# Seven block products instead of eight for the gate projection of a merge stage

## The chip, the cores and the metric

The kernel runs on one core of a Trainium2 chip, in float32 throughout. The metric is the device time of one execution in microseconds (us). PE is TensorE, PEld its weight loads, DVE VectorE, ACT ScalarE, POOL GpSimd, SP the engine whose queue issues most DMAs.

## The reference

A trunk of two layers over 512 latent tokens (layer 0 also carries 256 context tokens, so 768 in all; layer 1 has 512). Each layer runs a normalisation, a Hyena branch and an attention branch side by side, merges them, and then runs a mixture of experts. The change touches the merge alone:

```python
def merge_branches(p_gate, y_hy, y_att, w_hy_o, w_mla_o, w_out):
    g = jax.nn.sigmoid(p_gate)
    return (g[..., :D_MODEL] * (y_hy @ w_hy_o) + g[..., D_MODEL:] * (y_att @ w_mla_o)) @ w_out
```

`p_gate` is the normalised input `u` (tokens x 1024) times the last 2048 columns of `w_in`. `y_hy` and `y_att` have 512 columns each.

## The kernel before

The program is a row of stages. `stage` opens a block in which each engine has its own instruction list, and ends it with a barrier of all engines, so that no stage begins before the one ahead of it has ended on every engine. For each layer the order is: input projections, convolution, attention, merge (`merge_stage`), output projection and router logits (`out_stage`), router, experts.

Everything is held transposed: channels on the 128 partitions, tokens along the free dimension. `merge_stage` makes the 1024 output channels in 8 column chunks of 128, called c below (`KC` is 8). For a chunk it needs 16 weight tiles of 128x128 for the two gates (8 contraction chunks each) and 4 + 4 tiles for the two branch outputs. `merge_loads` fetches those 24 tiles into one of two halves of `w_merge`, in four DMAs. The halves for c = 0 and 1 are loaded during the attention stage; the half for c + 2 is loaded when TensorE has done with c.

For each chunk, TensorE works on each stream of tokens in turn (512 columns, and in layer 0 another 256): 8 + 8 matmuls for the gates and 4 + 4 for the branches, into four PSUM banks. ScalarE takes the sigmoid of the two gate banks (L1707), VectorE multiplies it by the two branch banks (L1719), GpSimd adds the two halves into `mix` (L1730). Two sets of four banks alternate. All of it stands in a `Fori` loop of 4 passes, each with both halves. Near the end SP issues the loads of `w_out`, which the next stage reads.

A float32 matmul shows in the trace as two records, each with a weight load of its own. One chunk is therefore 48 records for each stream.

Of the kernel before, what the change touches and what calls it, by code (L numbers as in the profile page):

```python
# [22 lines left out]
ACT = mybir.ActivationFunctionType  # L23
ALU = mybir.AluOpType
AX = mybir.AxisListType

P = 128
D = 1024
KC = D // P
SEQ, CTX = 512, 256  # L30
# [9 lines left out]
HC = HW // P  # L40
# [76 lines left out]
@contextmanager  # L117
def stage(nc, name, signals, buffers=()):

    with ExitStack() as ctx:  # L120
        mine = {n: ctx.enter_context(nc.sbuf_tensor(f"{name}_{n}", shape, dt[0] if dt else F32))
                for n, shape, *dt in buffers}
        sems = {n: nc.alloc_semaphore(f"{name}_{n}") for n in signals}
        with nc.Block() as block:
            yield block, {**mine, **sems}
        nc.clear_and_free_semaphores(list(sems.values()))
        nc.all_engine_barrier()  # L127
# [1531 lines left out]
def merge_loads(eng, l, i, b, a, early):  # L1659

    w, loaded = early
    for at, n, src, col in ((0, KC, a["w_in"], G0), (KC, KC, a["w_in"], G0 + D), (2 * KC, HC, a["w_hy_o"], 0),
                            (2 * KC + HC, HC, a["w_mla_o"], 0)):
        eng.dma_start(w[:, b, at:at + n], src[l].rearrange("(c p) n -> p c n", p=P)[:, :, bass.ds(i * (2 * P) + (b * P + col), P)]
                      ).then_inc(loaded[b], 16)


def merge_stage(nc, m, l, a, streams, early, then):

    NS = len(streams)  # L1670
    w, loaded = early
    with stage(nc, f"merge{l}", ["mm_done", "sig_done", "prod_done", "mix_done"],
               [("sig", [P, 2, 2, SEQ]), ("t", [P, 2, 2, SEQ])]) as (block, s):
        @block.sync
        def _(sp):
            with sp.Fori(1, KC // 2) as i:
                for b in range(2):
                    sp.wait_ge(s["mm_done"], i * (2 * NS) + (b + 1) * NS)
                    merge_loads(sp, l, i, b, a, early)
            then(sp)  # L1680

        @block.tensor
        def _(pe):
            pe.sem_inc(s["mm_done"], 2 * NS)
            with pe.Fori(0, KC // 2) as i:
                for b in range(2):
                    pe.wait_ge(loaded[b], i * 64 + 64)
                    for t, at, n in streams:
                        k = b * NS + t
                        pe.wait_ge(s["prod_done"], i * (2 * NS) + (k + 1))  # L1690
                        q = 4 * (k % 2)
                        for bank, w_at, z, kn in ((q, 0, m.u, KC), (q + 1, KC, m.u, KC), (q + 2, 2 * KC, m.yh, HC),
                                                  (q + 3, 2 * KC + HC, m.ya, HC)):
                            for c in range(kn):
                                last = nc.tensor.matmul(m.ps[:, bank, 0:n], w[:, b, w_at + c], z[:, c, at:at + n],  # L1695
                                                        start=c == 0, stop=c == kn - 1)
                        last.then_inc(s["mm_done"], 1)

        @block.scalar
        def _(act):  # L1700
            with act.Fori(0, KC // 2) as i:
                for b in range(2):
                    for t, at, n in streams:
                        k = b * NS + t
                        act.wait_ge(s["mm_done"], i * (2 * NS) + (k + 1 + 2 * NS))
                        act.wait_ge(s["prod_done"], i * (2 * NS) + (k + 1))
                        nc.scalar.activation(s["sig"][:, k % 2, :, 0:n], m.ps[:, 4 * (k % 2):4 * (k % 2) + 2, 0:n],  # L1707
                                             ACT.Sigmoid).then_inc(s["sig_done"], 1)

        @block.vector  # L1710
        def _(dve):
            dve.sem_inc(s["prod_done"], 2)  # L1712
            with dve.Fori(0, KC // 2) as i:
                for b in range(2):
                    for t, at, n in streams:
                        k = b * NS + t
                        dve.wait_ge(s["sig_done"], i * (2 * NS) + (k + 1))
                        dve.wait_ge(s["mix_done"], i * (2 * NS) + (k + 1))
                        nc.vector.tensor_tensor(s["t"][:, k % 2, :, 0:n], m.ps[:, 4 * (k % 2) + 2:4 * (k % 2) + 4, 0:n],  # L1719
                                                s["sig"][:, k % 2, :, 0:n], ALU.mult).then_inc(s["prod_done"], 1)  # L1720

        @block.gpsimd
        def _(pool):
            pool.sem_inc(s["mix_done"], 2)
            with pool.Fori(0, KC // 2) as i:
                for b in range(2):
                    for t, at, n in streams:
                        k = b * NS + t
                        pool.wait_ge(s["prod_done"], i * (2 * NS) + (k + 3))
                        nc.gpsimd.tensor_tensor(m.mix[:, bass.ds(i * 2 + b, 1), at:at + n].rearrange("p a n -> p (a n)"),  # L1730
                                                s["t"][:, k % 2, 0, 0:n], s["t"][:, k % 2, 1, 0:n], ALU.add).then_inc(s["mix_done"], 1)


def out_loads(eng, l, w_out, early):
# [132 lines left out]
def mixers(nc, m, l, a, consts, dram, late, begun):  # L1867
# [11 lines left out]
    with ExitStack() as whole, ExitStack() as until_qkv, ExitStack() as until_conv:  # L1879
# [52 lines left out]
        m.mix = late.enter_context(nc.sbuf_tensor(f"mix{l}", [P, KC, TOK], F32, side="right"))  # L1932
        out_early = late.enter_context(nc.sbuf_tensor(f"w_out{l}", [P, 2, KC, 4 * P], F32, side="right")), signals("w_out_in", 2)
        merge_stage(nc, m, l, a, streams, merge_early, lambda sp: out_loads(sp, l, a["w_out"], out_early))
    return out_early

# [682 lines left out]
```

## Time and profile before

| | |
|---|---|
| time, median of 3 runs | 2872.05 us (2866.27 to 2876.56) |
| span of the profiled execution | 2869.8 us |
| PE busy in it | 2557.7 us (89%) |
| DVE, ACT, POOL busy in it | 845.5, 610.8, 516.4 us |
| merge of layer 0, first to last PE record | from 725.7 us, 247.94 us busy |
| merge of layer 1, first to last PE record | from 2059.0 us, 165.06 us busy |

Times in the profile are microseconds from the start of the span. The time of the profiled execution itself, apart from its span, is not recorded; the span lies inside the range of the three runs, 2.25 us under their median.

### The profile page before, as it was taken

To read this page: it belongs to the slowest core of one execution; us is meant where nothing else is said; L and a number is where in the kernel's file an instruction comes from. 1 tells how busy PE (TensorE), PEld (TensorE's weight loads), DVE (VectorE), ACT (ScalarE), POOL (GpSimd) and SP (SyncE) were. 2 spreads that over 40 slices of the span, in tenths; PEclk is the share of its full clock that TensorE was granted. 3 is DMA by queue.
4 is the path that set the end of the run, shared out by engine and by line. 5 is a ranking of instruction groups with operands and counts; after the bars stand their busy time and mean duration, and the time that the engine had idled before them with its cause. 6 is when DMAs were issued, how large, how long until landed. Compare 5 with 4: busy or idle time off the path is not lost. (4 is left out here: it accounts for less than half of the span.)

```text
span 2869.8 us, 33789 instructions
## 1 busy us (share of the span) xinstructions
PE 2557.7 (89%) x12506; PEld 1481.5 (52%) x12506; DVE 845.5 (29%) x1651; ACT 610.8 (21%) x1195; POOL 516.4 (18%) x508
## 2 busy tenths in 40 slices
PE   7997999899999995999888689989999859988886
PEld 2445667555555543555555344755544445555553
DVE  5452257345000135221111142634300242211113
ACT  4342210145000011221111141014300112211111
POOL 0000001166000001222222200116400012222221
PEclk9998999899999997999999889989999979999998
DMA  9872220002023325999999913012033469999996
GB/s 356 294 290 76 74 103 15 20 13 51 23 66 102 125 94 232 388 401 399 402 395 386 357 62 124 30 24 58 1 88 102 182 265 400 389 402 408 400 406 235
DMA packets 208811, 590.78 MB, mean 206 GB/s; under 512 B 47360, under 2 KB 108843, under 8 KB 158412
## 3 DMA queue, kind: packets, MB, share of 16 engines
q1 hardware_dynamic: 185109, 557.75, 51.9%
q0 software_dynamic: 22944, 31.52, 3.3%
q8 instruction: 56, 0.92, 0.1%
q10 hardware_dynamic: 663, 0.27, 0.0%
q14 instruction: 39, 0.32, 0.0%
HBM read 584.07 MB, written 51.51 MB: 221 GB/s over the span
## 5 line engine op out<-in xcount | busy, mean ns | idle before, releaser
L2130 PE MATMUL ps<-w,moe_xt 128*64 128x256 f32 x4096 | 489.0, 393 | 96.4 <-DMA w<-in_w_up_e 94.4
L2130 PEld LDWEIGHTS ps<-w,moe_xt 128*64 128x64 f32 x4096 | 319.9, 141 | 221.1 <-issue 103.2
L2251 POOL DMA_INDIRECT rows_out<-moe_rows_out,table x128 | 118.3, 924 | 736.9 <-DVE moe_rows_out L2313 723.0
L2138 PE MATMUL ps<-w,moe_ht 128*64 128x512 f32 x1024 | 247.8, 605 | 1.6 <-issue 1.6
L2351 DVE TENSOR_TENSOR moe_gated<-ps,moe_gated 64x256 f32<-64x256 f32 x128 | 54.5, 426 | 541.5 <-ACT moe_gated L2332 541.5
L1695 PE MATMUL ps<-u,w_merge 128*128 128x256 f32 (+1 forms) x512 | 167.8, 486 | 2.2 <-DVEq L1712 2.2
L1452 POOL TENSOR_SCALAR attn_p<-attn_p,attn_rs 128x768 f32<-128x768 f32 (+1 forms) x80 | 155.1, 1946 | 81.5 <-DVE attn_rs L1621 81.1
L2313 DVE COPY moe_rows_out<-ps 64x512 f32<-64x512 f32 x128 | 88.7, 693 | 268.2 <-PE ps L2138 268.2
L2332 ACT ACTIVATE moe_gated<-ps 64x256 f32<-64x256 f32 x128 | 48.0, 375 | 549.7 <-PE ps L2130 549.7
L2146 PEld LDWEIGHTS ps<-ident,moe_xg 64*128 64x128 f32 x1024 | 122.5, 200 | 68.2 <-issue 68.2
L2146 PE MATMUL ps<-ident,moe_xg 64*128 64x64 f32 x1024 | 139.9, 277 | 19.1 <-DMA moe_xg<-rows_in,rows 19.0
L1791 PE MATMUL ps<-w_out,mix 128*128 128x512 f32 x320 | 144.6, 612 | 7.7 <-PEq L127 7.7
L1719 DVE TENSOR_TENSOR merge_t<-ps,merge_sig 128x1024 f32<-128x1024 f32 (+1 forms) x24 | 25.1, 1047 | 394.8 <-ACT merge_sig L1707 394.8
L1695 PEld LDWEIGHTS ps<-u,w_merge 128*128 128x128 f32 x512 | 97.2, 190 | 70.4 <-issue 61.2
L948 PE MATMUL ps<-u,w_hy 128*128 128x256 f32 (+1 forms) x384 | 127.1, 491 | 2.7 <-PEq L127 2.7
L2244 POOL DMA_INDIRECT moe_xg<-rows_in,rows x128 | 121.6, 950 | 43.1 <-issue 36.9
L1163 POOL TENSOR_TENSOR conv_u<-conv_u 128x1024 f32<-128x1024 f32 (+1 forms) x12 | 32.7, 2723 | 460.9 <-DVE conv_u L1187 460.9
L1695 PE MATMUL ps<-next_u,w_merge 128*128 128x512 f32 x256 | 111.3, 592 | 1.8 <-DVEq L1712 1.8
L2319 ACT ACTIVATE moe_rows_out<-ps 64x512 f32<-64x512 f32 x128 | 75.6, 590 | 172.5 <-PE ps L2138 172.5
L1791 PEld LDWEIGHTS ps<-w_out,mix 128*128 128x128 f32 x320 | 62.2, 196 | 85.1 <-issue 85.1
L2138 PEld LDWEIGHTS ps<-w,moe_ht 128*64 128x64 f32 x1024 | 62.4, 136 | 83.4 <-issue 74.8
L948 PEld LDWEIGHTS ps<-u,w_hy 128*128 128x128 f32 x384 | 73.0, 192 | 54.3 <-issue 49.9
(326 smaller groups left out, 3286.9 us busy)
## 6 DMA issues: line engine op xcount, KB each, us to landing
w<-in_w_gate_e SPq DMA_DIRECT2D x128, 1024.0 KB, 25.5
w<-in_w_up_e SPq DMA_DIRECT2D x128, 1024.0 KB, 29.5
w<-in_w_down_e SPq DMA_DIRECT2D x128, 1024.0 KB, 29.4
prep_w<-in_w_ada SPq DMA_DIRECT2D x24, 2048.0 KB, 13.3
w_merge<-in_w_in SPq DMA_DIRECT2D x32, 512.0 KB, 5.2
transfer<-prep_out POOLq DMA_DIRECT2D x10, 1024.0 KB, 6.2
y<-rows_out SPq DMA_DIRECT2D x20, 512.0 KB, 8.0
h<-transfer SPq DMA_DIRECT2D x4, 2048.0 KB, 11.5
```

Of the source, the lines that this page charges most:

```text
L948: last = nc.tensor.matmul(m.ps[:, 2 * (i % 2) + t, 0:n], w[:, (i // HC) % 2, c, (i % HC) * P:(i % HC + 1) * P], m.u[:, c, at:at + n], star ...
L1452: nc.gpsimd.tensor_scalar(p, p, s["rs"][:, u % 4:u % 4 + 1], None, ALU.mult).then_inc(s["norm_done"], 1)
L1695: last = nc.tensor.matmul(m.ps[:, bank, 0:n], w[:, b, w_at + c], z[:, c, at:at + n], start=c == 0, stop=c == kn - 1)
L1791: last = nc.tensor.matmul(m.ps[:, 2 * (j % 2) + half], m.mix[:, c, tile * P:(tile + 1) * P], w[:, half, c], start=c == 0, stop=c == KC - 1)
L2130: last = nc.tensor.matmul(ps[k * SLOTS:(k + 1) * SLOTS, 0:DE], xt[:, c], wgu[:, k, c], start=c == 0, stop=c == KC - 1)
L2138: last = nc.tensor.matmul(ps[k * SLOTS:(k + 1) * SLOTS, 0:512], ht[:, c], wd[:, c, k * 512:(k + 1) * 512], start=c == 0, stop=c == 1)
L2146: last = nc.tensor.transpose(ps[:, c * SLOTS:(c + 1) * SLOTS], src.rearrange("p (q c) -> p c q", c=n)[:, c], ident[0:SLOTS, 0:SLOTS])
L2244: nc.gpsimd.indirect_dma_start(out=xg[:, j % GR], out_offset=None, in_=dram["u"], in_offset=bass.IndirectOffsetOnAxis(ap=m.rows[0:SLOTS, j ...
L2251: nc.gpsimd.indirect_dma_start(out=dram["y"], out_offset=bass.IndirectOffsetOnAxis(ap=m.table[0:SLOTS, j:j + 1], axis=0), in_=y[:, j % 2], ...
L2313: copy(y[:, b % 2, half * 512:(half + 1) * 512], m.ps[half * SLOTS:(half + 1) * SLOTS, 5 + b % 2]).then_inc(sem, 1)
L2319: return nc.scalar.activation(out, in_, ACT.Copy)
L2351: nc.vector.tensor_tensor(h[:, b % 2], m.ps[SLOTS:2 * SLOTS, b % 2, 0:DE], sg[SLOTS:2 * SLOTS, b % 2], ALU.mult).then_inc(s["h_done"], 1)
```

## The change

`merge_stage` is written anew. The gate product of a chunk is a 2x2 block product: the contraction (1024) and the two gates give four weight blocks `a11, a12, a21, a22` of 4 tiles each, and the contraction and the tokens give four blocks `u11, u12, u21, u22`. H is half of the tokens: 384 in layer 0, 256 in layer 1. Both streams are taken together. `a11, a12` belong to the first gate and `a21, a22` to the second.

- Strassen's scheme (in Winograd's form) needs seven products of block sums: `p1` to `p7`, each 4 matmuls of H columns. Eight products were 16 matmuls for each stream.
- VectorE makes the sums of the `u` blocks once per layer (`t1` to `t4`, one of them in the place of `u12`).
- GpSimd makes the sums of the weight blocks for each chunk (`s1` to `s4`, `s3` in the place of `a21`), in front of the addition into `mix` of the chunk after.
- ScalarE copies `p1` and `p5` out of PSUM and takes four sigmoids of H columns; VectorE has seven additions of H columns per chunk that put the four result blocks together, and one multiplication of 4 x H columns by the four branch banks.
- The loop is unrolled, and 28 semaphores take the place of 4. The loads for c + 2 wait for `p4_done` and `branches_done` of c.
- For c = 0 the branch products come ahead of the gate products, otherwise behind them.

```diff
-                        for bank, w_at, z, kn in ((q, 0, m.u, KC), (q + 1, KC, m.u, KC), (q + 2, 2 * KC, m.yh, HC),
-                                                  (q + 3, 2 * KC + HC, m.ya, HC)):
-                            for c in range(kn):
-                                last = nc.tensor.matmul(m.ps[:, bank, 0:n], w[:, b, w_at + c], z[:, c, at:at + n],
-                                                        start=c == 0, stop=c == kn - 1)
+            def weight_sums(c):
+                a11, a12, a21, a22, s1, s2, s3, s4 = blocks(c)
+                pool.wait_ge(loaded[c % 2], 64 * (c // 2 + 1))
+                nc.gpsimd.tensor_tensor(s1, a21, a22, ALU.add).then_inc(s["s1_done"], 1)
+                pool.wait_ge(s["s1_done"], c + 1)
+                nc.gpsimd.tensor_tensor(s2, s1, a11, ALU.subtract).then_inc(s["s2_done"], 1)
+                pool.wait_ge(s["s2_done"], c + 1)
+                nc.gpsimd.tensor_tensor(s3, a11, a21, ALU.subtract).then_inc(s["s3_done"], 1)
+                nc.gpsimd.tensor_tensor(s4, a12, s2, ALU.subtract).then_inc(s["s4_done"], 1)
+            weight_sums(0)
+            weight_sums(1)
+            for c in range(KC):
+                mix(c)
+                if c + 2 < KC:
+                    weight_sums(c + 2)
...
+            def gate_products(c):
+                a11, a12, a21, a22, s1, s2, s3, s4 = blocks(c)
+                if c >= 1:
+                    pe.wait_ge(s["c11_done"], c)
+                product(X, a11, u11).then_inc(s["p1_done"], 1)
+                pe.wait_ge(s["s2_done"], c + 1)
+                if c == 0:
+                    pe.wait_ge(s["t2_done"], 1)
+                else:
+                    pe.wait_ge(s["u3_done"], c)
+                product(Y, s2, t2).then_inc(s["p6_done"], 1)
...
+                product(Z, s1, t1).then_inc(s["p5_done"], 1)
+                pe.wait_ge(s["p1_kept"], c + 1)
+                product(X, a12, u21).then_inc(s["p2_done"], 1)
+                pe.wait_ge(s["s3_done"], c + 1)
+                pe.wait_ge(s["u2_done"], c + 1)
...
+                product(Y, s3, t3).then_inc(s["p7_done"], 1)
+                pe.wait_ge(s["s4_done"], c + 1)
+                pe.wait_ge(s["p5_kept"], c + 1)
+                product(Z, s4, u22).then_inc(s["p3_done"], 1)
...
+                product(W, a22, t4).then_inc(s["p4_done"], 1)
...
+            def products(c):
+                dve.wait_ge(s["branches_done"], c + 1)
+                dve.wait_ge(s["sig_done"], 4 * c + 4)
+                g = gates(c)
+                nc.vector.tensor_tensor(g, m.ps[:, 4:8, 0:H], g, ALU.mult).then_inc(s["prod_done"], 1)
...
+                nc.vector.tensor_tensor(p1, m.ps[:, Y, 0:H], g[:, 1], ALU.add).then_inc(s["u3_done"], 1)
...
+                nc.vector.tensor_tensor(g[:, 1], g[:, 1], p5, ALU.add).then_inc(s["u4_done"], 1)
+                nc.vector.tensor_tensor(g[:, 3], p1, p5, ALU.add).then_inc(s["c22_done"], 1)
```

On TensorE, the first two visits of the loop in layer 0 before (one chunk, both streams; `yh` and `ya` are the two branch outputs):

```order
L1695 MATMUL ps<-u,w_merge 128x512 x16
L1695 MATMUL ps<-yh,w_merge 128x512 x4
L1695 MATMUL ps<-ya,w_merge 128x512 x4
L1690 REGISTER_ALU
L1695 MATMUL ps<-u,w_merge 128x256 x16
L1695 MATMUL ps<-yh,w_merge 128x256 x4
L1695 MATMUL ps<-ya,w_merge 128x256 x4
```

And the second chunk of the same layer now (`merge_s` holds s1, s2 and s4, `merge_t` t2, t3 and t4; t1 lies in `u`, s3 in `w_merge`):

```order
L1729 MATMUL ps<-u,w_merge 128x384 x4
L1729 MATMUL ps<-merge_t,merge_s 128x384 x4
L1729 MATMUL ps<-u,merge_s 128x384 x4
L1729 MATMUL ps<-u,w_merge 128x384 x4
L1729 MATMUL ps<-merge_t,w_merge 128x384 x4
L1729 MATMUL ps<-u,merge_s 128x384 x4
L1729 MATMUL ps<-merge_t,w_merge 128x384 x4
L1729 MATMUL ps<-yh,w_merge 128x384 x8
L1729 MATMUL ps<-ya,w_merge 128x384 x8
```

The chunk has gone from 24 matmuls of 512 columns and 24 of 256 to 44 of 384. On VectorE, from the start of the stage in layer 0, where the first row before was a `128x1024` multiplication, now stand the four sums t3, t1, t2, t4, then the additions of c = 0 (u2, c11, u3, u4, c22, c12, c21), then u2 of c = 1 and the multiplication of c = 0:

```order
L1807 TENSOR_TENSOR merge_t<-u 128x1536
L1809 TENSOR_TENSOR u<-u 128x4x384
L1811 TENSOR_TENSOR merge_t<-u 128x1536
L1813 TENSOR_TENSOR merge_t<-u,merge_t 128x1536
L1827 TENSOR_TENSOR merge_g<-ps,merge_p 128x384
L1831 TENSOR_TENSOR merge_g<-ps,merge_p 128x384
L1835 TENSOR_TENSOR merge_p<-ps,merge_g 128x384
L1838 TENSOR_TENSOR merge_g<-merge_g,merge_p 128x384
L1839 TENSOR_TENSOR merge_g<-merge_p 128x384
L1842 TENSOR_TENSOR merge_g<-ps,merge_g 128x384
L1844 TENSOR_TENSOR merge_g<-ps,merge_p 128x384
```

Two of these additions (L1838, L1839) and the four sums read both operands from SBUF. On GpSimd, which before had only the additions into `mix`, the weight sums of c = 1, the addition into `mix` of c = 0, and the sums of c = 2 stand like this:

```order
L1706 TENSOR_TENSOR merge_s<-w_merge 128x512
L1708 TENSOR_TENSOR merge_s<-merge_s,w_merge 128x512
L1710 TENSOR_TENSOR w_merge<-w_merge 128x512
L1711 TENSOR_TENSOR merge_s<-w_merge,merge_s 128x512
L1716 TENSOR_TENSOR mix<-merge_g 128x768
L1706 TENSOR_TENSOR merge_s<-w_merge 128x512
L1708 TENSOR_TENSOR merge_s<-merge_s,w_merge 128x512
```

The sums of a chunk now lie between its load and TensorE's second product of it.

## Rows read from the trace of the kernel before

**Rows 1.** The page: span, and busy time of each engine.

```profile
span 2869.8 us, 33789 instructions
PE 2557.7 (89%) x12506; PEld 1481.5 (52%) x12506; DVE 845.5 (29%) x1651; ACT 610.8 (21%) x1195; POOL 516.4 (18%) x508
```

**Rows 2.** Windows, merge records: stretch, length, PE, PEld, PEclk, DMA share, GB/s.

```profile
725.70:976.70 251.00, 247.94 (x768) 145.84 (x768) 1.00 0.20 54
2058.90:2228.60 169.70, 165.06 (x384) 72.88 (x384) 0.99 0.30 80
```

**Rows 3.** Timeline of PE, layer 0, third chunk: start, length, instructions.

```profile
756.79 13.90 PE L1695 MATMUL ps<-u,w_merge 128*128 128x512 f32 x32
...
777.39 7.07 PE L1695 MATMUL ps<-u,w_merge 128*128 128x256 f32 x32
784.29 1.89 PE L1695 MATMUL ps<-yh,w_merge 128*128 128x256 f32 x8
...
787.75 12.61 PE L1695 MATMUL ps<-u,w_merge 128*128 128x512 f32 x29
```

**Rows 4.** Timeline of PE, layer 1, heads of the second and third chunk.

```profile
2079.69 13.90 PE L1695 MATMUL ps<-next_u,w_merge 128*128 128x512 f32 x32
...
2100.29 4.03 PE L1695 MATMUL ps<-next_u,w_merge 128*128 128x512 f32 x9
```

**Rows 5.** Timeline of PE, convolution stage, groups that each wait at the head.

```profile
438.04 1.89 PE L1085 MATMUL ps<-v,conv_dft 128*128 128x256 f32 x8
439.77 3.62 PE L1123 MATMUL ps<-u,w_qkv 128*128 128x256 f32 x16
443.22 1.89 PE L1112 MATMUL ps<-conv_y,conv_idft 128*128 128x256 f32 x8
```

**Rows 6.** Timeline, start and end of the merge, layer 0.

```profile
725.73 3.69 PE L1695 MATMUL ps<-u,w_merge 128*128 128x512 f32 x8 [2.19 <-DVEq L1712]
...
973.79 0.60 ACT L1707 ACTIVATE merge_sig<-ps 128x512 f32<-128x512 f32 x1 [9.34 <-PE ps L1695]
...
975.29 0.72 POOL L1730 TENSOR_TENSOR mix<-merge_t 128x256 f32 x1 [8.13 <-DVE merge_t L1719]
...
976.78 1.17 PE L1791 MATMUL ps<-w_out,mix 128*128 128x512 f32 x1 [3.11 <-PEq L127]
```

**Rows 7.** Timeline, end of the merge, layer 1.

```profile
2220.45 3.60 PE L1695 MATMUL ps<-ya,w_merge 128*128 128x512 f32 x8
...
2224.17 1.02 ACT L1707 ACTIVATE merge_sig<-ps 128x1024 f32<-128x1024 f32 x1 [18.30 <-PE ps L1695]
2225.22 1.23 DVE L1719 TENSOR_TENSOR merge_t<-ps,merge_sig 128x1024 f32<-128x1024 f32 x1 [18.10 <-ACT merge_sig L1707]
2226.64 1.26 POOL L1730 TENSOR_TENSOR mix<-merge_t 128x512 f32 x1 [18.06 <-DVE merge_t L1719]
...
2228.66 1.19 PE L1791 MATMUL ps<-w_out,mix 128*128 128x512 f32 x1 [4.61 <-PEq L127]
```

**Rows 8.** The barrier ahead of layer 0's merge: count, ns min/median/max, start us.

```profile
L127 PEldq EVENT_SEMAPHORE  x1: 51/51/51, 725.1 to 725.1; - x1
```

**Rows 9.** Costs by line and shape: count, busy us, mean ns, idle before.

```profile
L1629 DVE COPY attn_pt<-ps 128x256 f32<-128x256 f32 x64 | 26.8, 419 | 29.3 <-PE ps L1513 29.3
L2390 DVE TENSOR_TENSOR moe_rows_out<-moe_incl,pick_iota 128x1664 f32<-128x1664 f32 x1 | 1.9, 1884 | 0.0
```

**Rows 10.** Timeline, convolution stage: VectorE and GpSimd both at SBUF operands.

```profile
404.41 4.51 DVE L1189 TENSOR_TENSOR conv_t<-conv_y,h 128x1024 f32<-128x1024 f32 x2
404.58 3.25 POOL L1163 TENSOR_TENSOR conv_u<-conv_u 128x1024 f32<-128x1024 f32 x1 [185.66 <-DVE conv_u L1187]
```

**Rows 11.** Loads of a half of `w_merge`: issue in layer 1, landing over all.

```profile
2080.05 1.02 SPq L1664 DMA_DIRECT2D w_merge<-in_w_in  x2
...
2082.39 0.69 SPq L1664 DMA_DIRECT2D w_merge<-in_w_mla_o  x1
DMA to landing us min/median/max: 4.0/5.3/7.6
```

More of the change, by code:

```diff
@@ L1668, in merge_stage, with blocks, gates @@
 def merge_stage(nc, m, l, a, streams, early, then):
-    NS = len(streams)
+    n_tok = sum(n for _, _, n in streams)
+    H, KH = n_tok // 2, KC // 2
     w, loaded = early
-    with stage(nc, f"merge{l}", ["mm_done", "sig_done", "prod_done", "mix_done"],
-               [("sig", [P, 2, 2, SEQ]), ("t", [P, 2, 2, SEQ])]) as (block, s):
+    X, Y, Z, W = range(4)
+    u = m.u
+    u11, u12, u21, u22 = (u[:, k * KH:(k + 1) * KH, n * H:(n + 1) * H] for k in range(2) for n in range(2))
+    with stage(nc, f"merge{l}", ["t1_done", "t2_done", "t3_done", "t4_done", "s1_done", "s2_done", "s3_done", "s4_done",
+                                 "p1_done", "p6_done", "p5_done", "p2_done", "p7_done", "p3_done", "p4_done", "branches_done",
+                                 "p1_kept", "p5_kept", "u2_done", "u3_done", "u4_done", "c11_done", "c12_done", "c21_done", "c22_done", "sig_done", "prod_done", "mix_done"],
+               [("t2", [P, KH, H]), ("t3", [P, KH, H]), ("t4", [P, KH, H]), ("s", [P, 2, 3, KH, P]),
+                ("p1", [P, 2, H]), ("p5", [P, 2, H]), ("g", [P, 2, 4, H])]) as (block, s):
+        t1, t2, t3, t4 = u12, s["t2"][:], s["t3"][:], s["t4"][:]
+        def blocks(c):
+            a11, a12, a21, a22 = (w[:, c % 2, k * KH:(k + 1) * KH] for k in range(4))
+            s1, s2, s4 = (s["s"][:, c % 2, k] for k in range(3))
+            return a11, a12, a21, a22, s1, s2, a21, s4
+        def gates(c):
+            return s["g"][:, c % 2]
@@ L1674, in _, with mix @@
         @block.sync
         def _(sp):
[L1676 to L1679, printed above, removed]
+            for c in range(2, KC):
+                sp.wait_ge(s["p4_done"], c - 1)
+                sp.wait_ge(s["branches_done"], c - 1)
+                merge_loads(sp, l, c // 2, c % 2, a, early)
             then(sp)
+        @block.gpsimd
+        def _(pool):
+            def weight_sums(c):
[7 more added lines that the diff above has]
+                nc.gpsimd.tensor_tensor(s4, a12, s2, ALU.subtract).then_inc(s["s4_done"], 1)
+            def mix(c):
+                pool.wait_ge(s["prod_done"], c + 1)
+                g = gates(c)
+                nc.gpsimd.tensor_tensor(m.mix[:, c, 0:n_tok].rearrange("p (h n) -> p h n", h=2), g[:, 0:2], g[:, 2:4], ALU.add).then_inc(s["mix_done"], 1)
+            weight_sums(0)
[4 more added lines that the diff above has]
+                    weight_sums(c + 2)
@@ L1682, in _, with product @@
         @block.tensor
         def _(pe):
[L1684 to L1691, printed above, removed]
-                        for bank, w_at, z, kn in ((q, 0, m.u, KC), (q + 1, KC, m.u, KC), (q + 2, 2 * KC, m.yh, HC),
-                                                  (q + 3, 2 * KC + HC, m.ya, HC)):
-                            for c in range(kn):
-                                last = nc.tensor.matmul(m.ps[:, bank, 0:n], w[:, b, w_at + c], z[:, c, at:at + n],
-                                                        start=c == 0, stop=c == kn - 1)
-                        last.then_inc(s["mm_done"], 1)
+            def product(bank, lhs, rhs):
+                for k in range(KH):
+                    ins = nc.tensor.matmul(m.ps[:, bank, 0:H], lhs[:, k], rhs[:, k], start=k == 0, stop=k == KH - 1)
+                return ins
@@ new lines, in gate_products @@
+            def gate_products(c):
[9 more added lines that the diff above has]
+                product(Y, s2, t2).then_inc(s["p6_done"], 1)
+                pe.wait_ge(s["s1_done"], c + 1)
+                if c == 0:
+                    pe.wait_ge(s["t1_done"], 1)
+                else:
+                    pe.wait_ge(s["c12_done"], c)
+                product(Z, s1, t1).then_inc(s["p5_done"], 1)
[3 more added lines that the diff above has]
+                pe.wait_ge(s["u2_done"], c + 1)
+                if c == 0:
+                    pe.wait_ge(s["t3_done"], 1)
+                product(Y, s3, t3).then_inc(s["p7_done"], 1)
+                pe.wait_ge(s["s4_done"], c + 1)
+                pe.wait_ge(s["p5_kept"], c + 1)
+                product(Z, s4, u22).then_inc(s["p3_done"], 1)
+                if c == 0:
+                    pe.wait_ge(s["t4_done"], 1)
+                else:
+                    pe.wait_ge(s["c21_done"], c)
+                product(W, a22, t4).then_inc(s["p4_done"], 1)
@@ new lines, in branches @@
+            def branches(c):
+                if c >= 1:
+                    pe.wait_ge(s["prod_done"], c)
+                for k, z in ((2 * KC, m.yh), (2 * KC + HC, m.ya)):
+                    for h in range(2):
+                        last = product(4 + (2 if z is m.ya else 0) + h, w[:, c % 2, k:k + HC], z[:, :, h * H:(h + 1) * H])
+                last.then_inc(s["branches_done"], 1)
+            for c in range(KC):
+                pe.wait_ge(loaded[c % 2], 64 * (c // 2 + 1))
+                if c == 0:
+                    branches(c)
+                gate_products(c)
+                if c:
+                    branches(c)
@@ L1699, in _, with sigmoid @@
         @block.scalar
         def _(act):
[L1701 to L1708, printed above, removed]
+            def sigmoid(out, in_):
+                nc.scalar.activation(out, in_, ACT.Sigmoid).then_inc(s["sig_done"], 1)
@@ new lines, in _ @@
+            for c in range(KC):
+                g, b = gates(c), c % 2
+                act.wait_ge(s["p1_done"], c + 1)
+                if c >= 2:
+                    act.wait_ge(s["c21_done"], c - 1)
+                    act.wait_ge(s["c22_done"], c - 1)
+                nc.scalar.activation(s["p1"][:, b], m.ps[:, X, 0:H], ACT.Copy).then_inc(s["p1_kept"], 1)
+                act.wait_ge(s["p5_done"], c + 1)
+                nc.scalar.activation(s["p5"][:, b], m.ps[:, Z, 0:H], ACT.Copy).then_inc(s["p5_kept"], 1)
+                act.wait_ge(s["c11_done"], c + 1)
+                sigmoid(g[:, 0], g[:, 0])
+                act.wait_ge(s["c22_done"], c + 1)
+                sigmoid(g[:, 3], g[:, 3])
+                act.wait_ge(s["c12_done"], c + 1)
+                sigmoid(g[:, 1], g[:, 1])
+                act.wait_ge(s["c21_done"], c + 1)
+                sigmoid(g[:, 2], g[:, 2])
@@ L1710, in _ @@
         @block.vector
         def _(dve):
[L1712 to L1731, printed above, removed]
+            nc.vector.tensor_tensor(t3, u22, u12, ALU.subtract).then_inc(s["t3_done"], 1)
@@ new lines, in _ @@
+            dve.wait_ge(s["t3_done"], 1)
+            nc.vector.tensor_tensor(t1, u12, u11, ALU.subtract).then_inc(s["t1_done"], 1)
+            dve.wait_ge(s["t1_done"], 1)
+            nc.vector.tensor_tensor(t2, u22, t1, ALU.subtract).then_inc(s["t2_done"], 1)
+            dve.wait_ge(s["t2_done"], 1)
+            nc.vector.tensor_tensor(t4, u21, t2, ALU.subtract).then_inc(s["t4_done"], 1)
+            def products(c):
+                dve.wait_ge(s["branches_done"], c + 1)
+                dve.wait_ge(s["sig_done"], 4 * c + 4)
+                g = gates(c)
+                nc.vector.tensor_tensor(g, m.ps[:, 4:8, 0:H], g, ALU.mult).then_inc(s["prod_done"], 1)
@@ new lines, in _ @@
+            for c in range(KC):
+                g, p1, p5 = gates(c), s["p1"][:, c % 2], s["p5"][:, c % 2]
+                dve.wait_ge(s["p6_done"], c + 1)
+                dve.wait_ge(s["p1_kept"], c + 1)
+                if c >= 2:
+                    dve.wait_ge(s["mix_done"], c - 1)
+                nc.vector.tensor_tensor(g[:, 1], m.ps[:, Y, 0:H], p1, ALU.add).then_inc(s["u2_done"], 1)
+                if c >= 1:
+                    products(c - 1)
+                dve.wait_ge(s["p2_done"], c + 1)
+                nc.vector.tensor_tensor(g[:, 0], m.ps[:, X, 0:H], p1, ALU.add).then_inc(s["c11_done"], 1)
+                dve.wait_ge(s["p7_done"], c + 1)
+                dve.wait_ge(s["u2_done"], c + 1)
+                dve.wait_ge(s["c11_done"], c + 1)
+                nc.vector.tensor_tensor(p1, m.ps[:, Y, 0:H], g[:, 1], ALU.add).then_inc(s["u3_done"], 1)
+                dve.wait_ge(s["u3_done"], c + 1)
+                dve.wait_ge(s["p5_kept"], c + 1)
+                nc.vector.tensor_tensor(g[:, 1], g[:, 1], p5, ALU.add).then_inc(s["u4_done"], 1)
+                nc.vector.tensor_tensor(g[:, 3], p1, p5, ALU.add).then_inc(s["c22_done"], 1)
+                dve.wait_ge(s["p3_done"], c + 1)
+                dve.wait_ge(s["u4_done"], c + 1)
+                nc.vector.tensor_tensor(g[:, 1], m.ps[:, Z, 0:H], g[:, 1], ALU.add).then_inc(s["c12_done"], 1)
+                dve.wait_ge(s["p4_done"], c + 1)
+                nc.vector.tensor_tensor(g[:, 2], m.ps[:, W, 0:H], p1, ALU.add).then_inc(s["c21_done"], 1)
@@ L1734, in out_loads @@
+            products(KC - 1)
 def out_loads(eng, l, w_out, early):
```

## Prediction

> **What bounds the kernel now.** I read the page first. PE is busy for 2557.7 of 2869.8 us, and the other engines for less than a third [rows 1]. The share of the whole says little about one stage, so I next took the merge records alone, in two windows. In layer 0 the 768 records fill 247.94 of the 251.0 us between the stage's first record and the next stage's; in layer 1, 384 records fill 165.06 of 169.7 us. PEclk, the granted clock, is 1.00 and 0.99, the upper level of 2.4 GHz, and the DMA engines are at 20 and 30% [rows 2]. So nothing but TensorE's columns counts inside this stage. What is left over is the start and the end, and there three other engines follow one another [rows 6, 7]. Every stage ends in a barrier of all engines, and no later stage uses anything that was started before the merge. A microsecond less here should be a microsecond less at the end, although the experts behind it wait partly on DMA.
>
> **What a column costs.** In the timeline the reader takes starts, not lengths, since ends are modelled. A chunk of layer 1, 48 records of 512 columns, takes 2100.29 - 2079.69 = 20.60 us [rows 4], 0.4292 each. In layer 0, 32 records of 256 go from 777.39 to 784.29, 0.2156 each, and a chunk takes 787.75 - 756.79 = 30.96 us [rows 3]. The cost is nearly proportional to the columns, and a record of 256 already hides its weight load. No record of 384 columns exists; I take the middle of the two, 0.3224 us. The bounds are the two straight readings, 1.5 x 0.2156 = 0.3234 and 0.75 x 0.4292 = 0.3219, which moves layer 0 by less than 0.8 us.
>
> One rule speaks against more and shorter matmuls. The Trainium skill (TensorE: Matmul & The Clock Gate, section The mechanism) lets a weight load overlap a running matmul only if the two use different row groups, and these use all rows. Were that so here, each of layer 1's 704 records would carry its load (72.88 us over 384, 0.19) in the open, and the stage would grow. The trace disagrees: 0.2156 us from start to start [rows 3] has no room for a load behind the matmul, so the measurement decides and the rule gets no chance.
>
> **The change, part by part.**
>
> *TensorE.* A chunk becomes 7 x 4 + 16 = 44 matmuls of H columns, 88 records. Layer 0: 88 x 0.3224 = 28.37 us, 2.59 less than 30.96; eight chunks give -20.7. Layer 1: 88 x 0.2156 = 18.97, or 19.03 by the pace of the convolution's groups (1.73 us for 8 records, [rows 5]); I take 19.0, 1.6 less than 20.60, and eight chunks give -12.8. Together -33.5 us.
>
> *The waits inside a chunk.* Call T one product of 8 records: 2.58 us in layer 0, 1.72 in layer 1, the tighter. Each of the banks X, Y, Z is used twice, 2T = 3.4 us apart. What must happen in between is one copy by ACT (under 0.60 us, the row of 512 columns, [rows 6]) or one addition by DVE (about 0.42, the price of 256 columns from PSUM, [rows 9]), plus 0.12 us of signalling (PE's last record ends at 2220.45 + 3.60 = 2224.05, ACT starts at 2224.17, [rows 7]). That leaves some 2.7 us of cover. Behind p7 DVE has u3, u4, c22, c12, c21: five times 0.42, and if GpSimd holds it up twice for 1.26, 4.6 us. That is 2.7T, while the first of them that TensorE needs next, u3, has 7T. The multiplication of chunk c-1 (4H = 1024 columns, 1.23 us, [rows 7]) comes behind u2 and must be done before `branches` at 7T; it is done by 2T + 1.8 us. All at nothing.
>
> *The weight sums.* They are new on the way from DMA to TensorE. In layer 1, from the release of a half, the last DMA issue starts 2.3 us after the first, and the slowest landing takes 7.6: 9.9 us [rows 11]. By then GpSimd is through with its `mix`, which comes ready at about 2T + 1.8 and takes 1.26 more. s1 and s2 are 2 x 1.26 = 2.5 us [rows 7], with a hold-up behind DVE at each about 4. So s2 stands at 14 us at the latest; TensorE wants it after 88 + 8 records, 20.7 us. Even at the price of the held-up 128x1024 row (3.25 for each, [rows 10]) it would be 16.4. In layer 0 the limit is 31 us. At nothing, with over 4 us of cover; without it each us late would cost one us, in six chunks of each layer.
>
> *The start.* t3, t1, t2 (DVE) and s1, s2 (GpSimd) are hidden by the 32 branch records and p1: 40 records, 12.9 us in layer 0 and 8.6 in layer 1. A sum of 4H columns is 1.75 us at 1536 (between 1.23 at 1024 and 1884 ns at 1664, [rows 7, 9]) and 1.23 at 1024. Both operands lie in SBUF on both engines, and for that there is a row: two DVE instructions of 1024 columns, 2.5 us at the price above, last 4.51 together beside a GpSimd one that runs from 404.58 to 407.83 [rows 10]. The second has waited for GpSimd's whole instruction. If the two take turns, t2 is ready at 3 x (1.75 + 1.26) = 9.0 us and 3 x (1.23 + 1.26) = 7.5 us, both in time. If GpSimd's eight sums all went first, it would be 10.1 + 5.3 = 15.4 and 10.1 + 3.7 = 13.8, and TensorE would stand for 2.5 + 5.2 = 7.7 us. GpSimd waits for its own semaphore twice in each chunk's sums, which lets DVE in, so I take turns: 0.
> The Trainium skill (SBUF — State Buffer, section Who interferes with whom) calls this pair of ports an exclusive lock that the loser waits out; the trace agrees, with the 4.51 us above.
>
> The other side of the start is a gain. PE is let go at the barrier at 725.1 + 0.05 [rows 8] and starts at 725.73, held by VectorE's first semaphore increment and the set-up of the loop [rows 6]. Neither is left. I take 0.5 us per layer, -1.0 (bounds 0 and -1.2).
>
> *The end.* Layer 0 before: from the sigmoid's start at 973.79 to the next stage's 976.78, with 0.12 us ahead of it, 3.1 us over 256 tokens [rows 6]. Now no sigmoid is left there, but the product is 1536 wide (1.75) and the addition 768 (0.72 at 256 and 1.26 at 512 give 1.81): 0.12 + 1.75 + 0.19 + 1.81 + 0.76 = 4.6, so +1.5; the gaps 0.19 and 0.76 are those of layer 1 [rows 7]. Layer 1 before: 2228.66 - 2224.05 = 4.6; now without the sigmoid's 1.02, -1.0. Sum +0.5. Clearing 28 semaphores I cost at 0: before, the clear is one instruction over a range.
>
> *Sum.* -33.5 - 1.0 + 0.5 = -34.0 us. Against the profiled span of 2869.8 that is 2835.8; that execution's own time isn't shown, and its span lies 2.25 us under the median of the runs, so I subtract from the median: 2838.0 us, 1.2% less. A difference of 0.3% (8.6 us) is about what a measurement of this kernel can tell from no change.
>
> **The rivals.**
>
> *GpSimd first at the start.* The 7.7 us above: 2845.7. For it: DVE's instruction did wait for a whole one of GpSimd [rows 10]. Against: it was let in after one. Chance 0.08.
>
> *Every wait costs a drain (the other side).* Each chunk has 8 groups with a wait at the head where layer 0 had two and layer 1 one: 128 against 24. If TensorE finished its work before it looked at the wait, each head would cost a semaphore's 0.12, an open weight load of 0.19 (145.84 us over 768, [rows 2]) and the fill of 0.17 (the last of 8 records lasts 3.60 - 7 x 0.429 = 0.60 against a pace of 0.43, [rows 7]): 0.48 us. 104 more of them are +50 and the result is 2888, slower. It decides from 34.0 / 104 = 0.33 us per head. Against it: heads at 777.39 and 787.75 follow at full pace [rows 3], and so do the convolution's, three in a row in groups of only 8 and 16 records, each head a wait [rows 5]. A tenth of the price would be +5, 2843. Chance 0.04 for the full price.
>
> *Late sums in every chunk.* If load and sums took 23 us instead of 14 in layer 1, TensorE would stand 2.3 us in six chunks, 14 us: 2852. Against: every row above. Chance 0.03. *Other:* unrolled code that arrives late, or a time behind the merge that doesn't move with it (the experts' DMA). The attention and convolution stages are unrolled and dense, and the experts' loads start behind the merge. A third of the gain lost, 2849: chance 0.05.
>
> *The forecast*, no stall worth naming: chance 0.8, 2831 to 2843 (the price of 384 columns +-0.8, the start, the end, and the runs' own scatter).
>
> **How the numbers follow.** 2838 is the likeliest case. The range goes up to take in the GpSimd case and a tenth-price drain, down by the scatter: 2830 to 2849. Faster by over 0.3% needs less than 2863.5, which all but the drain case and a part of the unknown give: 0.93. Same 0.03, slower 0.04.
>
> **What would show it.** In the merge's windows, about 227 and 152 us of PE records where there were 247.94 and 165.06, without gaps at the heads of the groups; records of 384 columns 0.322 us apart. t2 and s2 done before the 40th record. The last record to the next stage's first: 4.6 us in layer 0, 3.6 in layer 1. If the prediction is wrong, the list of waits for PE in the merge names the releaser: `t2` or `merge_s` for the start, `merge_s` in each chunk for late sums, and "issue" or PE's own queue for the drain.

## The result, and the profile after

The changed kernel takes 2839.89 us (2837.75 to 2842.11, four runs) against 2873.16 for the kernel before: ratio 0.989, 95% interval 0.9878 to 0.9901. The forecast was 2838.0. In the profile's page of the changed kernel the span is 33.8 us shorter, PE is busy for 30 us less, and DVE and POOL for 84 and 90 us more, beside the rows of before [rows 1]:

```profile
span 2836.0 us, 34353 instructions
PE 2527.3 (89%) x12762; PEld 1532.0 (54%) x12762; DVE 929.9 (33%) x1763; ACT 625.9 (22%) x1261; POOL 606.6 (21%) x564
```

Windows of the merge records alone (length, PE busy and records, PEld, PEclk, DMA share, GB/s):

```profile
722.00:951.00 229.00, 227.28 (x704) 133.68 (x704) 1.00 0.22 60
2018.00:2190.00 172.00, 152.19 (x704) 133.68 (x704) 1.00 0.30 80
```

Against [rows 2] that is 247.94 - 227.28 = 20.7 us in layer 0 and 165.06 - 152.19 = 12.9 in layer 1. The timeline of PE in layer 1, from the head of one chunk to that of the next, reads like this (start, length, instructions):

```profile
2094.06 1.89 PE L1729 MATMUL ps<-next_u,w_merge 128*128 128x256 f32 x8
2095.79 1.89 PE L1729 MATMUL ps<-merge_t,merge_s 128*128 128x256 f32 x8
2097.51 1.89 PE L1729 MATMUL ps<-next_u,merge_s 128*128 128x256 f32 x8
...
2106.15 3.62 PE L1729 MATMUL ps<-yh,w_merge 128*128 128x256 f32 x16
2109.60 3.62 PE L1729 MATMUL ps<-ya,w_merge 128*128 128x256 f32 x16
2113.05 1.24 PE L1729 MATMUL ps<-next_u,w_merge 128*128 128x256 f32 x5
```

The chunk takes 2113.05 - 2094.06 = 18.99 us, 0.216 for each of its 88 records, and the groups of 8 and 16 start 1.73 and 3.45 us apart. No row carries an idle time in brackets: none of the waits ahead of the groups is seen.

The start of layer 0's merge on all engines:

```profile
722.60 1.27 POOL L1706 TENSOR_TENSOR merge_s<-w_merge 128x512 f32<-128x512 f32 x1 [3.86 <-POOLq L127]
722.61 5.40 PE L1729 MATMUL ps<-yh,w_merge 128*128 128x384 f32 x16 [1.69 <-PEq L127]
722.61 2.87 DVE L1807 TENSOR_TENSOR merge_t<-u 128x1536 f32<-128x1536 f32 x1 [1.23 <-PEq L127]
723.95 2.66 POOL L1708 TENSOR_TENSOR merge_s<-merge_s,w_merge 128x512 f32<-128x512 f32 x1
725.52 2.71 DVE L1809 TENSOR_TENSOR u<-u 128x1536 f32<-128x1536 f32 x1
726.69 2.67 POOL L1710 TENSOR_TENSOR w_merge<-w_merge 128x512 f32<-128x512 f32 x1
...
728.26 2.71 DVE L1811 TENSOR_TENSOR merge_t<-u 128x1536 f32<-128x1536 f32 x1
...
735.59 2.74 PE L1729 MATMUL ps<-merge_t,merge_s 128*128 128x384 f32 x8
```

PE is held for 1.69 us by the barrier alone, 0.5 less than in [rows 6]. VectorE and GpSimd take turns, one instruction each, every 2.74 us (725.52 to 728.26 on VectorE). The block sum t2 (L1811) is there at 728.26 + 2.71 = 730.97, 8.4 us after the start, and the product that needs it starts at 735.59. The end of the same stage:

```profile
944.57 5.32 PE L1729 MATMUL ps<-ya,w_merge 128*128 128x384 f32 x16
949.93 1.76 DVE L1819 TENSOR_TENSOR merge_g<-ps,merge_g 128x1536 f32<-128x1536 f32 x1 [9.76 <-PE ps L1729]
951.77 1.80 POOL L1716 TENSOR_TENSOR mix<-merge_g 128x768 f32<-128x768 f32 x1 [20.95 <-DVE merge_g L1819]
...
954.50 2.90 PE L1905 MATMUL ps<-w_out,mix 128*128 128x512 f32 x3 [4.61 <-PEq L127]
```

4.61 us pass between the last record and the next stage's first. Cut at the first PE records of the stages, the two traces give this, in us:

| stretch | before | after | difference | forecast |
|---|---|---|---|---|
| start to merge, layer 0 | 725.73 | 722.61 | -3.1 | -0.5 |
| merge of layer 0, to the next stage | 251.05 | 231.89 | -19.2 | -19.2 |
| up to the merge of layer 1 | 1082.21 | 1082.50 | +0.3 | -0.5 |
| merge of layer 1, to the next stage | 169.67 | 155.72 | -14.0 | -13.8 |
| rest | 641.14 | 643.28 | +2.1 | 0 |

The first row holds more than the change can do: in twelve profiles, of these two kernels and the experiments below, that stretch lay anywhere between 720.9 and 726.4 us, so it is scatter. The last row scatters too, between 640.8 and 644.1 us in the same twelve. The two merge rows give -19.16 - 13.95 = -33.1 us where -33.0 was forecast. The other three miss by -2.6, +0.8 and +2.1 us and nearly cancel, so it is luck that the whole span comes within 0.2 us of the forecast sum of -34.0; a sum has to be checked stage by stage.

### The profile page after: what moved, and what is told of

Read it like the earlier page. It is cut to its first block and busy times, and to the rows that moved or that the text cites. A ratio compares the mean times of both kernels' runs of the same rounds, so it can differ in the third digit from the quotient of the medians.

```text
span 2836.0 us, 34353 instructions
## 1 busy us (share of the span) xinstructions
PE 2527.3 (89%) x12762; PEld 1532.0 (54%) x12762; DVE 929.9 (33%) x1763; ACT 625.9 (22%) x1261; POOL 606.6 (21%) x564
## 5 line engine op out<-in xcount | busy, mean ns | idle before, releaser
L2433 ACT ACTIVATE moe_xt<-ps 128x512 f32<-128x512 f32 x128 | 76.5, 597 | 100.2 <-PE ps L2260 100.2
L2260 PEld LDWEIGHTS ps<-ident,moe_gated 64*128 64x128 f32 x256 | 39.9, 203 | 103.2 <-issue 103.1
L948 PE MATMUL ps<-next_u,next_w_hy 128*128 128x512 f32 x192 | 86.2, 605 | 2.6 <-PEq L127 2.6
L1716 POOL TENSOR_TENSOR mix<-merge_g 128x768 f32<-128x768 f32 (+1 forms) x16 | 24.6, 1536 | 258.7 <-DVE merge_g L1819 258.7
```

Of the source, the lines that this page charges most:

```text
L948: last = nc.tensor.matmul(m.ps[:, 2 * (i % 2) + t, 0:n], w[:, (i // HC) % 2, c, (i % HC) * P:(i % HC + 1) * P], m.u[:, c, at:at + n], star ...
L2260: last = nc.tensor.transpose(ps[:, c * SLOTS:(c + 1) * SLOTS], src.rearrange("p (q c) -> p c q", c=n)[:, c], ident[0:SLOTS, 0:SLOTS])
L2433: return nc.scalar.activation(out, in_, ACT.Copy)
```

## Experiments

Each is an edit of the changed kernel. The ratios are to the kernel before, measured beside each. The changed kernel was measured once more, to compare the others with:

> The changed kernel once more, as the mark for the others of this call. Both theories: 0.9885 of before, within 0.1%.

Measured: 2841.80 us, ratio 0.9894 (0.9879 to 0.9909). In one place its profile differs from the first one. Layer 0's merge begins like this:

```profile
723.93 8.34 PE L1729 MATMUL ps<-yh,w_merge 128*128 128x384 f32 x16 [1.69 <-PEq L127]
732.11 5.32 PE L1729 MATMUL ps<-ya,w_merge 128*128 128x384 f32 x16
```

The same 16 records take 732.11 - 723.93 = 8.18 us where the first profile has 727.85 - 722.61 = 5.24, behind the same idle time of 1.69 us. The granted clock was 0.50 in the 4 us from 723.9 and 1.00 at that place in the other eleven profiles. So one profile in twelve loses 2.9 us inside the merge, and single profiles of one kernel differ by as much.

**Is it the columns?**

```diff
+                product(W, a22, t4)
                 product(W, a22, t4).then_inc(s["p4_done"], 1)
```

> The product of a22 and t4 is done twice for each chunk, so that TensorE has the columns of eight products again, and the block sums, the unrolled code, the start and the end stay as changed. If the gain is the columns alone: 8 records more per chunk, 8 x 8 x 0.3224 = 20.6 us in layer 0 and 8 x 8 x 0.216 = 13.8 in layer 1, 34.4 us over the changed kernel, so level with before (ratio to before 1.000). If a part of the gain came from the unrolled code or from taking both streams together: clearly faster than before, under 0.997.

Measured: 2874.25 us, ratio 1.0006 (0.9997 to 1.0015), 32.5 over the changed kernel measured beside it (34.4 were expected). From the first to the last merge record the stages grew by 20.6 and 13.8 us over the changed kernel's first profile, as worked out. In the timeline of PE the row with the doubled product has 16 records where the others have 8, at the same pace:

```profile
2088.83 1.89 PE L1729 MATMUL ps<-next_u,merge_s 128*128 128x256 f32 x8
2090.55 3.62 PE L1729 MATMUL ps<-merge_t,w_merge 128*128 128x256 f32 x16
2094.01 3.62 PE L1729 MATMUL ps<-yh,w_merge 128*128 128x256 f32 x16
```

With eight products' worth of columns the whole gain is gone. Unrolling, the joined streams and the other engines' new work carry nothing that this measurement can see.

**Do met waits cost?** The rival with the drain, tested by adding waits:

```diff
                 for k in range(KH):
+                    nc.tensor.wait_ge(loaded[0], 64)
                     ins = nc.tensor.matmul(...)
```

> Each of the 352 matmuls of a merge waits for a semaphore that has long been raised (the first load of w_merge). If a wait that is already met costs TensorE nothing while its queue is full: the time of the changed kernel within 0.2%, and records of 256 columns still 0.216 us apart. If each costs a drain of 0.48 us: some 590 more heads, 280 us more. If only the sequencer's 0.05 us showed: 30 us more.

Measured: 2839.74 us, ratio 0.9892 (0.9875 to 0.9908), the changed kernel's time. Timeline of PE, layer 1:

```profile
2077.35 1.89 PE L1730 MATMUL ps<-merge_t,merge_s 128*128 128x256 f32 x8
2079.08 1.89 PE L1730 MATMUL ps<-next_u,merge_s 128*128 128x256 f32 x8
```

1.73 us for eight records, still 0.216 each, with a wait at every one of the 704 matmuls of the two merges. The trace records 126 of the added waits as instructions of their own, at the heads of groups that had a wait already; those at the other 578 matmuls leave no record, so for them the time alone speaks. A wait that is met in time is free here.

**Does the start need its cover?**

```diff
-                if c == 0:
-                    branches(c)
                 gate_products(c)
-                if c:
-                    branches(c)
+                branches(c)
```

> For c = 0 too the gate products come ahead of the branch products, so that the first block sums lie in the open. If GpSimd and VectorE take turns at SBUF as in the changed kernel's trace (t2 ready 8.4 us after the first record in layer 0, 6.8 in layer 1): TensorE waits before its second product for 8.4 - 2.6 = 5.8 us and 6.8 - 1.7 = 5.1 us, 10.9 us over the changed kernel, and up to 3 more if the granted clock falls. If the turns cost nothing (t2 at 5.3 and 3.7 us): 2.7 + 2.0 = 4.7 us.

Measured: 2855.55 us, ratio 0.994 (0.9927 to 0.9954), 13.8 over the changed kernel measured beside it. Timeline of PE in both layers, and the windows behind the waits (length, PE, PEld, DVE, ACT, POOL busy, PEclk, DMA, GB/s):

```profile
734.84 4.85 PE L1729 MATMUL ps<-merge_t,merge_s 128*128 128x384 f32 x8 [5.67 <-DVE merge_t L1808]
...
2056.25 3.53 PE L1729 MATMUL ps<-merge_t,merge_s 128*128 128x256 f32 x8 [4.92 <-DVE merge_t L1808]
```

```profile
734.80:738.80 4.00, 3.96 (x6) 2.19 (x7) 2.63 (x1) 0.00 (x0) 3.92 (x3) 0.50 0.00 0
2056.10:2059.10 3.00, 2.85 (x7) 2.30 (x8) 2.17 (x1) 0.00 (x0) 3.00 (x2) 0.56 0.00 0
```

The waits are 5.67 and 4.92 us, 10.6 in sum, where 10.9 were expected. The rest is the clock, for which the expectation had allowed up to 3 us: after each wait the granted clock is 0.50 to 0.56, that is the lower level of 1.2 GHz, and eight records take 4.68 us from start to start (734.84 to 739.52) in place of 2.58.

**Why were the first sums long?**

```diff
+            pool.wait_ge(s["t4_done"], 1)
             weight_sums(0)
```

> GpSimd waits for VectorE's last block sum before its first weight sum. If the long first instructions (2.71 us for 1536 columns, 2.13 for 512 on GpSimd) are each other's doing: VectorE's four sums take 1.75 and 1.23 us each, GpSimd's 1.27, and TensorE still waits for nothing, since s2 is there at 7.0 + 2.7 = 9.7 us against 12.9 in layer 0 and 4.9 + 2.7 = 7.6 against 8.6 in layer 1. If the operands or the place in memory make them long: the same 2.7 as before.

Measured once: 2837.1 us. Timeline of DVE and POOL, layer 0:

```profile
722.76 1.76 DVE L1808 TENSOR_TENSOR merge_t<-u 128x1536 f32<-128x1536 f32 x1 [1.22 <-PEq L127]
724.56 1.76 DVE L1810 TENSOR_TENSOR u<-u 128x1536 f32<-128x1536 f32 x1
...
729.99 1.27 POOL L1706 TENSOR_TENSOR merge_s<-w_merge 128x512 f32<-128x512 f32 x1 [11.08 <-DVE merge_t L1814]
731.33 1.27 POOL L1708 TENSOR_TENSOR merge_s<-merge_s,w_merge 128x512 f32<-128x512 f32 x1
```

1.76 and 1.27 us for the same instructions that took 2.71 and 2.66 together. The long times were each other's doing, and TensorE waited for neither order. t2 comes sooner this way and s2 later (732.60); in layer 1 s2's cover is down to about 1 us.

**How much cover have the weight sums?** The same edit with two counts, for the chunks 2 to 7:

```diff
+                for x in range(N if c >= 2 else 0):
+                    pool.wait_ge(s["s1_done"], c + 1)
+                    nc.gpsimd.tensor_tensor(s4, a21, a22, ALU.add).then_inc(s["extra"], 1)
+                    pool.wait_ge(s["extra"], N * (c - 2) + x + 1)
```

> Four more sums in the same place, 5.4 us. Cycle 12.9 us against 19.0, and the first sum (after the load) in time by 4.6 us: no change from the changed kernel, in either layer. If the cover is smaller than worked out: up to 5.4 us in each of 12 chunks.

Measured with N = 4: 2839.94 us, ratio 0.9894 (0.9878 to 0.9911). No change.

> Twelve more sums of 128x512 on GpSimd (into s4, which is written anew afterwards) between s1 and s2 of the chunks 2 to 7, each 1.27 us and 0.08 for its wait: 16.2 us. If the sums have cover in layer 1 up to the second product and cost one us for each us beyond it: GpSimd's cycle from p6 of one chunk over its mix to s2 of the next is 3.5 + 1.3 + 18.9 = 23.7 us against 19.0, first stall 6.2 and then five of 4.7, 30 us more in layer 1 and nothing in layer 0 (25.9 against 28.4): 1.0% over the changed kernel. If GpSimd slows TensorE also where nobody waits for it: more than 30, in layer 0 too.

Measured with N = 12: 2878.13 us, ratio 1.0019 (1.0009 to 1.0029), 38 over the changed kernel. (One of its ten executions took 10130.59 us; nothing recorded shows why, and the ratio leaves it out.) Layer 0's merge was as long as in the changed kernel (226.8 us from its first to its last record's start); layer 1's grew from 151.8 to 191.6. The list of waits for PE in layer 1's merge, then a piece of the timeline, then two windows of it:

```profile
PE ps L1733 <- POOL merge_s L1712: 25.9, 6, 5.7
```

```profile
2105.75 1.89 PE L1733 MATMUL ps<-next_u,w_merge 128*128 128x256 f32 x8
2111.90 3.78 PE L1733 MATMUL ps<-merge_t,merge_s 128*128 128x256 f32 x8 [4.25 <-POOL merge_s L1712]
2115.47 3.07 PE L1733 MATMUL ps<-next_u,merge_s 128*128 128x256 f32 x8
```

```profile
2086.30:2090.00 3.70, 3.69 (x9) 2.97 (x10) 0.00 (x0) 0.00 (x0) 2.48 (x2) 0.50 0.00 0
2090.00:2100.00 10.00, 10.00 (x47) 8.78 (x46) 5.75 (x8) 1.97 (x5) 7.84 (x7) 0.97 0.00 0
```

The waits came where they were expected, six of them, 25.9 us in sum against 29.7. The other 14 us are again the clock: 3.57 us for eight records after a wait, where 1.73 is the pace. What was missing in my expectation is that these stalls cost about half as much again afterwards.

**The end, and the clock behind it.** This raised the question what TensorE's idle time at the end of the merge costs in the next stage. One kernel makes the end short, the other keeps TensorE busy through it. The short end finishes the last chunk in pieces on VectorE (not shown: GpSimd has no last addition, and TensorE signals the halves of the last branch product earlier):

```diff
+            c, g = KC - 1, gates(KC - 1)
+            dve.wait_ge(s["sig_done"], 4 * KC)
+            dve.wait_ge(s["part_done"], 1)
+            nc.vector.tensor_tensor(g[:, 0:2], m.ps[:, 4:6, 0:H], g[:, 0:2], ALU.mult).then_inc(s["quarter_done"], 1)
+            for h in range(2):
...
+                nc.vector.tensor_tensor(g[:, 2 + h], m.ps[:, 6 + h, 0:H], g[:, 2 + h], ALU.mult).then_inc(s["quarter_done"], 1)
+                dve.wait_ge(s["quarter_done"], 2 + h)
+                nc.vector.tensor_tensor(m.mix[:, c, h * H:(h + 1) * H], g[:, h], g[:, 2 + h], ALU.add).then_inc(s["mix_done"], 1)
```

> The last chunk of each layer is finished in pieces: the multiplication for the first branch while TensorE does the second, then one half of the tokens at a time, and the addition into mix on VectorE. If the time from the last record to the next stage's first is what counts: 4.6 us become 0.12 + 0.56 + 0.07 + 0.56 + 0.76 = 2.1 in layer 0, and 3.5 become 1.8 in layer 1, 4.2 us less than the changed kernel (0.15%). If the barrier waits for something else: no change.

Measured: 2831.53 us, ratio 0.9861 (0.9846 to 0.9876), 10.3 under the changed kernel measured beside it, where 4.2 were expected. The other kernel:

```diff
+            pe.wait_ge(s["c11_done"], KC)
+            product(X, w[:, 1, 0:KH], u11)
```

> The changed kernel with four more matmuls (a product that nobody reads) behind the last branch product of each layer, so that TensorE does not stand while VectorE and GpSimd finish. Its idle time before the next stage falls from 4.6 and 3.5 us to about 2.0 and 1.8, while the tail from the last useful record stays 4.6 and 3.5 us. If the shorter idle time keeps the granted clock up (it was 1.00 in the kernel with the shorter tail and 0.50 to 0.59 in the changed one in the next stage's first 4 us): about 4 us less than the changed kernel, ratio to before 0.9875 where the changed one has 0.989. If the clock there has another cause, or the gain of the shorter tail was the tail alone: no change, 0.989.

Measured: 2833.93 us, ratio 0.9867 (0.9851 to 0.9884).

> The kernel with the shorter tail once more. Tail (4.2 us) and clock (about 4 us) together: 8 us under the changed kernel, ratio to before 0.986. If its first result was scatter: 0.9875, for the tail alone.

Measured: 2832.02 us, ratio 0.9857 (0.9841 to 0.9874). That is under the changed kernel's 0.989 and 0.9894, with intervals that don't meet; from the kernel with the extra product, 1.9 us away, it can't be told.

The windows of 4 us from the next stage's first record, layer 0 and layer 1. The changed kernel (PEclk is 0.50 and 0.57; the columns are PE, PEld, DVE, ACT, POOL, PEclk, DMA, GB/s):

```profile
954.40:958.40 4.00, 3.90 (x5) 1.84 (x6) 0.00 (x0) 0.00 (x0) 0.00 (x0) 0.50 0.72 211
2192.60:2196.60 4.00, 3.88 (x5) 1.70 (x6) 0.00 (x0) 0.00 (x0) 0.00 (x0) 0.57 0.51 199
```

The kernel with the short end, and below it the one with the extra product (PE alone, PEclk, DMA, GB/s):

```profile
950.20:954.20 4.00, 3.94 (x9) 1.00 0.69 240
2185.70:2189.70 4.00, 3.91 (x9) 1.00 0.72 202
```

```profile
952.80:956.80 4.00, 3.89 (x9) 1.00 0.48 195
2189.40:2193.40 4.00, 3.95 (x10) 1.00 0.66 221
```

Nine or ten records in 4 us where there were five. In their timelines PE has idled for 2.12 and 2.03 us ahead of layer 0's next stage, against 4.61 above:

```profile
950.26 25.13 PE L1918 MATMUL ps<-w_out,mix 128*128 128x512 f32 x58 [2.12 <-PEq L127]
```

```profile
952.91 5.39 PE L1907 MATMUL ps<-w_out,mix 128*128 128x512 f32 x12 [2.03 <-PEq L127]
```

The changed kernel has 51 records in its first 25 us there and 54 in layer 1, the short end 58 in both: 7 + 4 records of 0.43 us, 4.7 us. But not all of that reaches the end of the stage. From its first record to its last the stage takes 102.9 and 66.1 us in the changed kernel, 101.7 and 64.4 with the short end (in both of its profiles), 100.0 and 64.4 with the extra product. In layer 0 the short end gives back 1.7 us further on, where one more of the later groups is slow:

```profile
981.86 13.95 PE L1918 MATMUL ps<-w_out,mix 128*128 128x512 f32 x32
...
999.63 15.64 PE L1918 MATMUL ps<-w_out,mix 128*128 128x512 f32 x32
```

In the second of them, behind 1.1 us of idle time and a row of short matmuls, the granted clock was 0.50 (window 1000.00 to 1003.00). So the traces place 2.5 + 1.7 us of the short end's gain in the ends and 1.3 + 1.7 in the stages behind, 7.1 together. The ratios say 0.3 to 0.4%, 8 to 11 us; the rest is placed nowhere, and the stretch behind layer 1's merge scatters by 3 us from profile to profile. The extra product leaves the ends as long as they were and saves 4.6 us in the stages behind. Measured it is 7 us by the medians (0.9867 against 0.989 and 0.9894), with intervals that overlap a little, so its size is less sure than the clock in the windows.

## Why the prediction was right

- **TensorE's columns.** Forecast -20.7 and -12.8 us; the windows gave -20.7 and -12.9. Records of 384 columns take (227.28 us over 704) 0.323 us, between the two bounds of 0.3219 and 0.3234. (The prediction says that no record of 384 columns existed. Layer 0's router stage had four, L2001 and L2002, at 0.85 to 0.93 us each, too few and too slow to give a pace.) That the time is nearly proportional to columns from 256 to 512 was the one assumption that carried the sum, and adding the eighth product back cost the whole gain.
- **The waits inside a chunk** were costed at nothing and are nothing: not one idle time of PE in the steady state, and 704 further met waits changed nothing. The rival with a drain per wait falls.
- **The weight sums.** Costed at nothing with over 4 us of cover. Measured, s2 stands at 2066.95 in layer 1 for a product that starts at 2076.79, so the cover is 9.8 us; 5.4 us more of sums in each chunk were free, 16.2 were not. The rival of late sums falls, and the place at which it would have decided is now known.
- **The start.** I took turns between VectorE and GpSimd, t2 at 9.0 and 7.5 us. They took turns, at 8.4 and 6.8. The rival, GpSimd first, falls. The gain of 0.5 us per layer from the vanished loop set-up was there: PE's idle time ahead of the merge went from 2.19 and 1.80 us to 1.69 and 1.32.
- **The end.** Forecast 4.6 and 3.6 us from last record to next stage; measured 4.61 and 3.54. So +1.5 and -1.0, as summed.
- **What the working missed.** It took the stages behind the merge as fixed. The next stage in fact begins at the lower clock, before and after alike. By the records in its first 25 us (58 at the upper clock) it loses 1.7 and 2.1 us in the kernel before (54 and 53) and 3.0 and 1.7 in the changed one (51 and 54). The two sides lose nearly the same, so the forecast came out right without this term; that is luck, since nothing in the working made them equal. It also left out that the merge itself can begin at the lower clock, 2.9 us in one profile of twelve. In the expectations for the experiments the same gap shows: 4.2 became 8 to 11, and 30 became 38; 10.9 became 13.8, within the 3 us that were allowed for the clock there.

The measured gain by ratio is 31.6 us (28.4 to 35.0) and by the medians 33.3; the sum had 34.0.

## What to carry to other kernels

Where one engine is busy without a gap, the profile's pace per column and a count of columns give the gain of that stage to a microsecond, and what other engines take over costs nothing as long as each deadline is written down beside the row of what must meet it. A scheme of seven products instead of eight pays where the sums have such cover; here it was 1.1% of the kernel, and 17% more busy time for GpSimd. Look at the ends of such a stage as well: about two microseconds less of TensorE standing still, in each layer, were worth 3.0 us (short end) to 4.6 us (extra product) in the two stages behind.

## What the runs showed of the hardware

- What the granted clock did after TensorE had been idle, at the starts of the merges and of the stages behind them and at the stalls of two experiments, in all twelve profiles: after 3.1 to 5.7 us of idle time it was 0.50 to 0.61 over the next 4 us in 25 of 26 places, and eight records of 384 columns took 4.68 us in place of 2.58 behind one of them. After 1.3 to 2.2 us it was 1.00 in 29 of 30 places. The exceptions are the start of the merge above (1.69 us idle, 0.50) and, in the run without cover, the stage behind layer 1's merge:

```profile
2211.93 8.39 PE L1902 MATMUL ps<-w_out,mix 128*128 128x512 f32 x19 [3.54 <-PEq L127]
```

Here the 4 us from 2211.9 had 1.00 behind the same 3.54 us of idle time after which the changed kernel had 0.57. The slow group of the short end above began behind 1.1 us. So the granted clock goes with the length of the idle time, and isn't settled by it alone. The Trainium skill (TensorE: Matmul & The Clock Gate, section Why this matters for your kernels) advises against idle gaps between matmul bursts for this reason; the windows above agree, the two exceptions apart.
- Beside each other, a VectorE instruction with two SBUF operands (1.76 us alone) and a GpSimd one (1.27) come round every 2.74 us, 0.3 less than their sum, in layer 1 every 2.2 against 1.23 + 1.27 = 2.5. They exclude each other for most of their length, not for all of it: the lock of which the prediction speaks is measured 0.3 us looser. Each shows in the trace at 2.66 to 2.87 us, where it took 1.76 or 1.27 alone: its wait is counted as its own time, and a long mean there is a sign of the other engine.
